# Woven linear attention on one core: gating a group's two heads at two places of VectorE's order instead of one

## The reference, cut to what matters

```
gla_o = rms_norm(gla_o.transpose(0, 2, 1, 3), g_gla).reshape(B, T, GLA_V_W) * jax.nn.silu(parts[6])
```

## Time and profile before

| what | value |
|---|---|
| median of 3 runs | 2662.31 us (2661.5, 2662.31, 2666.17) |
| the profiled execution | 2665.78 us, its span 2664.0 us |
| TensorE busy | 2603.6 us, 98% of the span |
| VectorE busy | 1560.5 us, 59% |
| ScalarE, GpSimd busy | 762.7 us and 619.8 us |
| mean granted TensorE clock | 0.994 |

### The profile page before, as it was taken

One profiled execution on the slowest core, in us unless ns is written; L12 is line 12 of the kernel. 1 busy time (PEld: TensorE's weight loads), 2 busy tenths in 40 slices (PEclk: granted clock), 3 DMA queues, 4 the chain that ended last, 5 costly groups with the idle time before them and its releaser, 6 DMA issues.

```text
span 2664.0 us, 36760 instructions
## 1 busy us (share of the span) xinstructions
PE 2603.6 (98%) x14360; PEld 2162.8 (81%) x14360; DVE 1560.5 (59%) x2453; ACT 762.7 (29%) x1293; POOL 619.8 (23%) x600
## 2 busy tenths in 40 slices
PE   6999999999999999999999999999999999999998
PEld 5888888888888877877777779988778888888887
DVE  5545554454544446247675579977448666666665
ACT  3100000000000024233345568872123222222224
POOL 1064466565440000003440027560000000000001
PEclk8999999999999999999999999999999999999999
DMA  6322112222221103112224310005401111111122
GB/s 238 110 68 68 63 52 84 91 78 93 82 68 41 39 19 120 52 60 61 72 73 125 100 48 1 2 17 179 137 16 48 47 63 55 55 47 47 47 63 87
DMA packets 198294, 187.75 MB, mean 70 GB/s; under 512 B 7645, under 2 KB 149770, under 8 KB 198026
## 3 DMA queue, kind: packets, MB, share of 16 engines
q1 hardware_dynamic: 190160, 171.83, 20.3%
q10 hardware_dynamic: 7994, 13.97, 1.4%
HBM read 161.39 MB, written 24.38 MB: 70 GB/s over the span
## 4 chain that ended last, share of the span: by engine, by line
PE 91%; DVE 4%; ACT 2%; DMA 1%; issue 1%; ACTq 0%; POOL 0%; SPq 0%; DVEq 0%; POOLq 0%
PE psum L222 21%; PE psum L223 21%; PE psum L224 21%; PE psum L1120 5%; PE psum L1122 5%; PE psum L1123 5%; PE psum L2441 3%; PE psum L2461 1%; PE psum L2460 1%; PE psum L2415 1%; PE psum L2416 1%; PE psum L2051 1%; PE psum L544 0%; DVE wh L197 0%; DVE wl L199 0%
## 5 line engine op out<-in xcount | busy, mean ns | idle before, releaser
L222 PE MATMUL psum<-nh,wh 128*128 128x512 f32 (+2 forms) x1688 | 629.9, 373 | 6.0 <-DVE nl L595 4.9
L223 PE MATMUL psum<-nl,wh 128*128 128x512 f32 (+2 forms) x1688 | 615.3, 365 | 0.0
L224 PE MATMUL psum<-nh,wl 128*128 128x512 f32 (+2 forms) x1688 | 614.2, 364 | 0.0
L222 PEld LDWEIGHTS psum<-nh,wh 128*128 128x128 f32 (+1 forms) x1688 | 318.0, 188 | 71.5 <-issue 10.7
L223 PEld LDWEIGHTS psum<-nl,wh 128*128 128x128 f32 (+1 forms) x1688 | 318.0, 188 | 52.7 <-issue 4.1
L224 PEld LDWEIGHTS psum<-nh,wl 128*128 128x128 f32 (+1 forms) x1688 | 317.7, 188 | 52.8
L222 PE MATMUL psum<-hidh,wh 128*128 128x512 f32 (+1 forms) x880 | 328.7, 374 | 3.5 <-DVE h L925 3.0
L223 PE MATMUL psum<-hidl,wh 128*128 128x512 f32 (+1 forms) x880 | 324.9, 369 | 0.0
L224 PE MATMUL psum<-hidh,wl 128*128 128x512 f32 (+1 forms) x880 | 323.9, 368 | 0.0
L197 DVE CAST wh<-raw 128x1024 fp32r<-128x1024 f32 (+1 forms) x111 | 84.7, 763 | 322.5 <-PE psum L224 322.4
L892 ACT ACTIVATE silu_a<-psum 128x512 f32<-128x512 f32 (+1 forms) x66 | 34.7, 527 | 827.1 <-PE psum L224 827.1
(11 more groups left out here) (351 smaller groups left out, 4750.9 us busy)
## 6 DMA issues: line engine op xcount, KB each, us to landing
raw<-in_w_ffn_up_dram SPq DMA_DIRECT2D x88, 512.0 KB, 3.9
mod_part<-in_w_mod_dram SPq DMA_DIRECT2D x96, 256.0 KB, 4.2
raw<-in_w_ffn_down_dram SPq DMA_DIRECT2D x44, 512.0 KB, 3.5
raw<-in_w_in_dram SPq DMA_DIRECT2D x34, 512.0 KB, 3.9
mod_raw<-in_w_mod_dram SPq DMA_DIRECT2D x12, 1024.0 KB, 10.8
gates_saved<-staged ACTq DMA_DIRECT2D x40, 256.0 KB, 2.0
merge_gate<-gates_saved SPq DMA_DIRECT2D x8, 1024.0 KB, 5.2
x_rows<-in_x_dram SPq DMA_DIRECT2D x8, 512.0 KB, 8.3
```

Of the source, the lines that this page charges most:

```text
L222: pe.matmul(o, hi_w, hi_x, start=first, stop=False)
L223: pe.matmul(o, hi_w, lo_x, start=False, stop=False)
L224: return pe.matmul(o, lo_w, hi_x, start=False, stop=last)
```

## The change

The gating of a group is taken apart by head. The first head (`par` = 0) stays at `OUT_SLOTS[g] + 5`. The second (`par` = 1) moves to `OUT_SLOTS[g] + 7`, that is to half-units 95, 104, 113 and 122. The instructions, their operands and their semaphores are the same; the wait on `z_loaded` is now made at both places. Since `gla_store(g)` waits for both heads, it too comes later.

```
-        if h - 5 in OUT_SLOTS:
-            g = OUT_SLOTS.index(h - 5)
-            dve.wait_ge(z_loaded, 16 + 32 * (g + 1))
-            for par in range(2):
+        for par, later in ((0, 5), (1, 7)):
+            if h - later in OUT_SLOTS:
+                g = OUT_SLOTS.index(h - later)
+                dve.wait_ge(z_loaded, 16 + 32 * (g + 1))
                 dve.wait_ge(o_rs, 2 * g + par + 1)
                 dve.wait_ge(g_oc, 2 * g + par + 1)
                 nc.vector.scalar_tensor_tensor(gla_f[:, par, :], gla_f[:, par, :], cols_b[:, B_GGLA:B_GGLA + 1],
```

## The result

The changed kernel takes 2669.12 us (median of 20 runs, 2665.67 to 2672.39) against 2663.06 us before (20 runs). The ratio is 1.0022, 95% interval 1.0016 to 1.0028: 5.9 us slower, where 4.2 was forecast. The profiled execution has a span of 2670.1 us, 6.1 more than before. In three kernels of the experiments one run each (3234, 3236 and 6661 us) stood far off all others, and the ratios given there leave it out.

A forecast was written before the change was run, and what follows sets the result against it. TensorE, busy 98% of the span, was taken as the bound. Groups 0 to 3 summed as -2.6 + 0.5 + 0 + 6.3 = +4.2 us on 2662.3, giving 2666.5 us, range 2662.0 to 2670.5.

The forecast's parts named there:

- Group 0: Half-units 93 to 95: item 13 starts earlier on TensorE, a gain of about 2.6 us.
- clock kept: Group 0, behind item 13's shorter wait: TensorE's clock stays up, a gain of 3.0 us.
- clock lost: Group 0, behind item 13's shorter wait: TensorE's clock still falls, a gain of 2.1 us.
- Group 1: Half-units 102 to 104: the 1.38 us wait goes but is handed back by the output products; loss of about 0.5 us.
- Group 2: Half-units 111 to 113: the pair goes behind item 30's products and the split starts at the same time; no change.
- Group 3: Half-units 120 to 122: late store delays the table loads, so VectorE and TensorE wait; loss of about 6.3 us.
- The stall: Group 3: TensorE's permutation waits for VectorE's normalising in half-unit 123, delayed by the late table; 5.1 us.
- The clock: Group 3: TensorE's clock falls after its new wait of about 5 us; cost 2.1 us.
- The waits that I took off: Group 3: TensorE's later wait at 1443.61 goes (0.55 us), and about 0.35 us on the way to the sum.
- the table stays hidden: Rival: VectorE does not stand still in half-unit 122, group 3 costs nothing; -2.1 us, 2660.2 us, chance 0.07.
- GpSimd conflicts cost whole instructions: Rival: VectorE and GpSimd exclude each other fully in groups 0 and 1; +5.3 us, 2667.6 us, chance 0.12.
- The fourth rival: Table lands later and low clock lasts: group 3 loses 7.9, group 0 gains 2.1; +6.3 us, 2668.6 us, chance 0.24.

The follow-up runs named there:

- group 1 only: Against the kernel before, only group 1's second head moved, to half-unit 104; 2664.02 us, ratio 1.0003.
- group 0 only: Against the kernel before, only group 0's second head moved, to half-unit 95; 2661.94 us, ratio 0.9996.
- table early: Changed kernel with table loads ahead of the last store and the last group's second gate values in cum; 2661.91 us, ratio 0.9994 against before.
- first three groups: Against the kernel before, second heads of groups 0 to 2 moved, the last one's stayed at half-unit 120; 2660.40 us, ratio 0.9987.
- panel 29 late: Changed kernel with the load of panel 29 waiting until the rotation table has landed; 2669.12 us, ratio 1.0023 against before.
- last-group-only kernel: Against the kernel before, only the last group's second head moved, to half-unit 122; 2672.02 us, ratio 1.0031.
- all moved by one half-unit: Against the kernel before, all four second heads moved one half-unit later, to 94, 103, 112 and 121; 2659.87 us, ratio 0.9988.
- 95 with 103: Against the kernel before, group 0's second head at half-unit 95, group 1's at 103, others unmoved; 2658.26 us, ratio 0.9984.
- table alone late: Kernel before, no gating moved, with the two table loads waiting for the split of panel 27; 2665.88 us, ratio 1.0015.

## Why the prediction was right

**The form.** A gain at group 0, nearly nothing at groups 1 and 2, and a larger loss at group 3 through the table: all four are seen in the stages and, apart from group 2, in a kernel of their own. The time, 2669.1, is in the range of 2662.0 to 2670.5. Forecast +4.2, measured +5.9, past the 5.3 us that the prediction took as the least it could tell from no change; its chance for that was 0.40. In the profiles the four stages make +4.9, and that this lies near +4.2 is in part luck: group 3 lost 1.8 more than forecast, group 0 gained 0.8 more and group 1 lost 0.3 less.

**Group 0**: forecast -2.6. The wait of item 13 fell from 3.41 to 2.17 us (said: 2.2). Of the two cases, clock kept and clock lost, priced at 3.0 and 2.1, the stages show 3.4 and 2.2. The new wait at item 15 was 0.46 where 0.7 was put. Both cases occur. A kernel with the second head in its old place varies as well: behind the same 3.4 us of wait stage 0 took 22.19 us in its own profile and 21.21 in that of group 1 only, where this code is the same. So the gain is anything from 1.2 (20.00 against 21.21) to 3.4 us in a pair of executions, and its mean is not shown more closely than by the runs: -1.1 (group 0 only), -1.6 (table early) and -3.5 (first three groups), with intervals that overlap.

**Group 1**: forecast +0.5, measured +0.2, with the wait handed back at the output products (1.31), where it was said, and at item 23 (0.46), which the prediction did not name. The idle time of VectorE that opened ahead of item 22 was 0.61 us (said 0.65), and its 0.95 us ahead of the split is gone. From the first head's gating to the last merge VectorE took 18.15 us for 17.94, so the conflicts cost 0.21 + 0.95 - 0.61 = 0.55 us, where 0.85 was put. So moving work inside a stretch that VectorE fills moved nothing; moving it by one half-unit gave 1.1 us, since it then fills that idle time and is clear of GpSimd.

**Group 2**: forecast 0, measured -0.1. VectorE waited 0.20 us for TensorE ahead of the split (0.16 before).

**Group 3**: forecast +6.3, measured +8.1. The mechanism was right (table late, 6.85 us on VectorE, TensorE held at the second permutation). Two terms of the sum were mis-sized. The stall was put at 5.1 and was 5.82 us, for two reasons. I took the table as complete at 1432.9, from the first load's issue and the median landing. The longer of the two times with the later issue, 1427.7 + 5.8, gives 1433.5, so there was 0.7 us of slack and not 1.3, and the 8.9 us then lead to 1442.4. Groups 0 to 2 put everything 2.9 us earlier (1407.40 against 1404.49), so that is 1439.5 in the changed kernel's count, and VectorE's row starts at 1439.56. The other 0.2 us I took off because no store of ScalarE would run beside the loads; but its next one was issued at 1437.14, in their midst. The other blame I had ready, the panel load behind the table, was tried and is not it. The clock was put at 2.1 us: the way from the permutation to the sum took 6.62 us for 3.79, so 2.8; with panel 29 late it was 6.52 - 3.79 = 2.7 and in the last-group-only kernel 5.55 - 3.79 = 1.8. The waits that I took off (0.55 and 0.35) were 0.56 and 0.1.

**The rivals.** That the table stays hidden is refuted by the wait itself and becomes true only with the loads in front of the store. That GpSimd conflicts cost whole instructions is not borne out: group 1 lost 0.2 us and not 1.1, and VectorE's slowed instructions again took 1.0 to 1.1 us against 0.7. GpSimd's beside them were held too: 1.06 us each, for 0.61 alone, so each engine paid part of the turns they took. The Trainium skill's rule (page "SBUF — State Buffer", section "SBUF: two separate sides") holds here in kind; a whole GpSimd instruction would have added 0.61 us, and 0.3 to 0.4 were added. The fourth rival, a later table and a longer low clock, comes nearest: 7.9 against 8.1 for group 3, and +6.3 against +5.9 in all. Of its two causes the longer low clock was there (2.8 for its 2.7) and the panel load was not; and the clock that it let fall at group 0 stayed up in the changed kernel's profile.

## What to carry to other kernels

An instruction that nobody waits for is free only together with all that stands behind its semaphore. Here it was the store, and behind the store, on the same queue, two loads that had nothing to do with it but their place in the order; so follow each queue past the waiting DMA up to its first consumer, for every repetition of a pattern and above all for the last one. When one edit moves four copies of a pattern, judge each copy by its own neighbours: one gained 1 to 3 us, one lost 8, and a choice per copy beat both kernels.

## What the runs showed of the hardware

The same wait of TensorE can cost its clock or not. At item 13 it stood idle for 2.2 us in seven profiles with the same work ahead of it; the granted clock over the stretch around it was 1.00 in four (the changed kernel, panel 29 late, all moved by one half-unit, and 95 with 103) and 0.88 in three (first three groups, table early, group 0 only). Up to this point the changed kernel and those with panel 29 late and the table early run the same instructions, so it is not an edit that decides. A wait of 3.4 us cost it in all four profiles that had it (before, last group only, group 1 only, table alone late), but not the same: from item 13 to item 14 TensorE then took 6.62 to 6.74 us in three and 5.64 in group 1 only, for 4.04 at full clock. The wait of 1.9 us at about 1185, from which the prediction took its price, was followed by a mean clock of 0.72 over 6 us in nine of the eleven profiles and of 1.00 in two (all moved by one half-unit, and panel 29 late). Two rows of the same stretch, first the changed kernel and then the first three groups:

```profile
1300.00:1314.00 14.00, 11.69 (x80) 8.87 (x76) 13.90 (x18) 5.13 (x10) 7.42 (x8) 1.00 0.31 99
```

```profile
1300.00:1314.00 14.00, 11.80 (x77) 9.27 (x77) 12.47 (x17) 5.33 (x10) 5.64 (x7) 0.88 0.23 71
```

The difference is 1.2 us of stage 0 (18.83 against 20.00), a third to a half of what the change gained there, so an effect of that size needs many runs and not one profile.
